# The last 64 tokens of a PEER layer leave the dense down product for gathered value rows

## The chip, the cores and the metric

The kernel runs on one core of a Trainium2 chip, as one launch. The metric is the time of one execution on the device in microseconds (us). The host lays the inputs out by tiles before the launch and is not timed.

## The reference, cut to what matters

Two layers work on 512 tokens of width 1024. Each layer is a convolution and pooling mixer, then a PEER layer: every token picks 8 x 16 = 128 of 16384 one-neuron experts, and its result is the weighted sum of their value rows.

```python
best_v, best_j = lax.top_k(comb, PEER_TOPK)            # 16 per head, 8 heads
idx = (i1 * N_KEYS + i2).astype(jnp.int32)             # expert numbers, 0..16383
gate = jax.nn.softmax(best_v, axis=-1)
...
a = jnp.einsum("tmd,td->tm", u_tab[ib], xb)            # activation of each picked expert
wgt = gb * jax.nn.gelu(a, approximate=False)
return jnp.einsum("tm,tmd->td", wgt, v_tab[ib])        # sum of 128 weighted value rows
```

## The kernel before, in words

The kernel computes the PEER layer densely. The 16384 experts are 128 chunks of 128. In the **up stage** each chunk's tile of `u` (128 x 1024, 512 KB) is multiplied with all 512 tokens; ScalarE applies GELU and stores the result, `[128 experts, 512 tokens]`, in DRAM (`ga_dram`). In the **down stage** each chunk's activations come back, are multiplied with a gate matrix that is zero wherever a token didn't pick the expert, and the product with the chunk's tile of `v` is added up in the eight PSUM banks, one for each 128 of the 1024 output columns.

All of these products are in split precision. A float32 operand is a high half (`_hi`, rounded to fp32r) and a low half (`_lo`, the rest), and a product is three matmuls: high x high, high x low, low x high. So one chunk is 24 matmuls of 128 x 128 weights against 512 tokens: 16 with `w_hi` (L439 in the up stage, L563 in the down stage) and 8 with `w_lo` (L443, L567). The last chunk of a down stage is at L586. ScalarE makes `w_hi` (helper `hi`, L598), GpSimd or VectorE makes `w_lo` (L782 on GpSimd; L1122 and L1149 on VectorE). The tiles of `u` and `v` arrive in a ring of four buffers (`ring`); `w_hi`, `w_lo`, `v_hi`, `v_lo` have two buffers each.

The up stage has four parts. While VectorE finds the best 16 of each head (`top16`, L1059 to L1063, and the gathers at L1093 to L1096), 40 chunks run (`RETRIEVING`). Eight more follow (`EARLY` is 48), beside which TensorE transposes indices and gates (L531) and VectorE copies them out (L1110 to L1115). In the next 64 chunks (`LATE`) the gate matrix is also built: for each of `TOK` = 8 tokens a chunk, VectorE writes one-hot rows (L1129, L1131), TensorE multiplies them (16 small matmuls at L546), ScalarE copies the result (L740) and stores it in blocks of 64 tokens (`g_dram`, `GBLOCKS` = 8). In these 64 chunks VectorE makes `w_lo` (L1122); in the last 16 chunks GpSimd does.

In the down stage SP issues, for each chunk, the activations (L308, 256 KB), the gates (L309, 256 KB, in runs of 64 tokens, which are 256 B) three chunks ahead (`load_back`), and the tile of `v` (`load_tile`, L260). In layer 0 it also issues the next layer's adaLN weights (L332, 512 KB, two in every round of four chunks, over the first 24 rounds), which VectorE reduces with `modulate` (L832). VectorE works in program order (`weights`): the product of activation and gate (L1140), `v_hi` (L1144), `v_lo` (L1146), `w_lo` (L1149). TensorE may start a chunk when `v_lo` of it is there (semaphore `w_ready`). At a stage's end VectorE adds the banks to `x` (L1167).

## Time and profile before

| | |
|---|---|
| median of 3 runs | 3599.91 us (3596.28 to 3601.85) |
| the profiled execution | 3602.71 us, its span 3600.7 us |
| TensorE matmul busy | 3503.5 us, 97% of the span, 16668 instructions |
| VectorE busy | 2422.0 us, 67% |
| ScalarE busy | 1039.3 us, 29% |
| GpSimd busy | 438.8 us, 12% |
| DMA | 633.62 MB, mean 176 GB/s |

The span is the time between the first and the last recorded instruction. A matmul's recorded duration (389 ns for the forms of a chunk) is from its start to the end of its result, and overlaps the next one's; the pace is the distance of starts, or the length of a run of matmuls in the chain of waits divided by their number. The down stage of layer 0 runs from about 1109 to 1813 us of the span, that of layer 1 from about 2884 to 3579 us.

### The profile page before, as it was taken

Reading aid. Unit: us, or ns where it says so; the run is one execution under the profiler, and the core shown is the slowest. Engines: PE = TensorE matmul, PEld = TensorE weight load, DVE = VectorE, ACT = ScalarE, POOL = GpSimd, SP = SyncE. Lnnn points to the kernel's source line nnn. Section 1 sums busy time; section 2 is a strip of 40 time slices with the busy share of each in tenths; the row PEclk is TensorE's granted clock in tenths of the full one; section 3 lists DMA queues with packets and bytes.
Section 4 is the critical chain, followed back from the end, with each engine's and each line's share of the span. In section 5 each row is a group of like instructions: output and inputs, shape, how many; then the busy total and the mean of one; then the engine's idle time right before and its main releaser. Section 6 shows DMA issues by size and latency. Waiting matters only on the chain.

```text
span 3600.7 us, 56122 instructions
## 1 busy us (share of the span) xinstructions
PE 3503.5 (97%) x16668; PEld 2836.9 (79%) x16668; DVE 2422.0 (67%) x6622; ACT 1039.3 (29%) x1382; POOL 438.8 (12%) x186
## 2 busy tenths in 40 slices
PE   5999999999999999999999999999999999999998
PEld 3578888888887888888875788888888888888886
DVE  6973996999924666665577159969999055555555
ACT  3333223444432212121242332234444312121122
POOL 0033443000031000000001334410000400000000
PEclk8999999999999999999999999999999999999999
DMA  6152443555547777786621224435555566666663
GB/s 221 58 215 90 146 143 138 186 199 216 216 181 222 243 235 243 243 244 195 181 93 37 78 97 143 146 132 216 216 181 204 204 204 193 193 192 195 190 196 119
DMA packets 442868, 633.62 MB, mean 176 GB/s; under 512 B 285984, under 2 KB 286368, under 8 KB 440352
## 3 DMA queue, kind: packets, MB, share of 16 engines
q1 hardware_dynamic: 402752, 495.60, 43.5%
q10 hardware_dynamic: 40032, 137.07, 9.7%
q8 instruction: 32, 0.52, 0.1%
q14 instruction: 52, 0.43, 0.0%
HBM read 496.26 MB, written 136.31 MB: 176 GB/s over the span
## 4 chain that ended last, share of the span: by engine, by line
PE 78%; DVE 16%; issue 3%; DMA 1%; ACT 1%; DVEq 0%; SPq 0%; ACTq 0%
PE bank L563 26%; PE bank L439 22%; PE bank L567 13%; PE bank L443 11%; PE bank L546 3%; DVE z_pad L1095 2%; DVE h L1060 2%; DVE h L1063 2%; DVE h L1062 1%; DVE h L1059 1%; DVE scratch L969 1%; DVE z_pad L1093 1%; DVE h L1096 1%; DVE u_pad L1061 1%; PE bank L362 1%
## 5 line engine op out<-in xcount | busy, mean ns | idle before, releaser
L598 ACT ACTIVATE w_hi<-ring 128x1024 fp32r<-128x1024 f32 x584 | 618.9, 1060 | 2243.0 <-PE bank L567 1110.7
L439 PE MATMUL bank<-h_hi,w_hi 128*128 128x512 f32 x2528 | 1000.3, 396 | 5.1 <-ACT scratch L598 2.3
L439 PE MATMUL bank<-h_lo,w_hi 128*128 128x512 f32 x2528 | 985.8, 390 | 0.0
L563 PE MATMUL bank<-v_hi,w_hi 128*128 128x512 f32 x2032 | 792.1, 390 | 5.7 <-DVE v_lo L1146 5.7
L563 PE MATMUL bank<-v_lo,w_hi 128*128 128x512 f32 x2032 | 791.8, 390 | 0.0
L782 POOL TENSOR_TENSOR w_lo<-ring,w_hi 128x1024 fp32r<-128x1024 f32 x172 | 437.1, 2543 | 1717.1 <-ACT w_hi L598 1717.1
L443 PE MATMUL bank<-h_hi,w_lo 128*128 128x512 f32 x2528 | 624.2, 389 | 0.0
L439 PEld LDWEIGHTS bank<-h_hi,w_hi 128*128 128x128 f32 x2528 | 474.8, 188 | 105.1 <-ACT w_hi L598 4.9
L443 PEld LDWEIGHTS bank<-h_hi,w_lo 128*128 128x128 f32 x2528 | 474.5, 188 | 98.5
L439 PEld LDWEIGHTS bank<-h_lo,w_hi 128*128 128x128 f32 x2528 | 474.9, 188 | 97.2 <-issue 1.4
L1131 DVE TENSOR_SCALAR h<-iota_b,keys 128x128 f16<-128x128 f16 x2048 | 543.5, 308 | 0.0
L567 PE MATMUL bank<-v_hi,w_lo 128*128 128x512 f32 x2032 | 501.8, 389 | 0.0
L1144 DVE CAST v_hi<-scratch 128x512 fp32r<-128x512 f32 x256 | 109.2, 427 | 580.7 <-PE bank L567 555.3
L563 PEld LDWEIGHTS bank<-v_hi,w_hi 128*128 128x128 f32 x2032 | 382.5, 188 | 85.8 <-DVE v_lo L1146 6.2
L563 PEld LDWEIGHTS bank<-v_lo,w_hi 128*128 128x128 f32 x2032 | 382.1, 188 | 79.3
L567 PEld LDWEIGHTS bank<-v_hi,w_lo 128*128 128x128 f32 x2032 | 381.4, 188 | 79.2
L1149 DVE TENSOR_TENSOR w_lo<-ring,w_hi 128x1024 fp32r<-128x1024 f32 x256 | 313.7, 1225 | 0.0
L1140 DVE TENSOR_TENSOR scratch<-scratch 128x512 f32<-128x512 f32 x256 | 175.1, 684 | 156.5 <-DMA scratch<-g_scratch 156.5
L1129 DVE TENSOR_SCALAR h<-iota_b,keys 128x128 f16<-128x128 f16 x1024 | 253.4, 247 | 0.0
L1122 DVE TENSOR_TENSOR w_lo<-ring,w_hi 128x1024 fp32r<-128x1024 f32 x128 | 156.7, 1224 | 68.8 <-ACT w_hi L598 68.7
L1146 DVE TENSOR_TENSOR v_lo<-scratch,v_hi 128x512 fp32r<-128x512 f32 x256 | 177.3, 692 | 8.8
L740 ACT ACTIVATE scratch<-bank 128x512 f32<-128x512 f32 x256 | 139.1, 596 | 82.1 <-ACT norm_tmp L710 82.1
(147 smaller groups left out, 1990.9 us busy)
## 6 DMA issues: line engine op xcount, KB each, us to landing
ring<-u_t SPq DMA_DIRECT2D x256, 512.0 KB, 3.3
ring<-v_t SPq DMA_DIRECT2D x256, 512.0 KB, 3.4
ga_scratch<-norm_tmp ACTq DMA_DIRECT2D x256, 256.0 KB, 2.0
g_scratch<-scratch ACTq DMA_DIRECT2D x16, 4096.0 KB, 13.4
scratch<-ga_scratch SPq DMA_DIRECT2D x256, 256.0 KB, 3.8
scratch<-g_scratch SPq DMA_DIRECT2D x256, 256.0 KB, 4.2
scratch<-ada_t SPq DMA_DIRECT2D x76, 512.0 KB, 5.3
ring<-wq_t SPq DMA_DIRECT2D x32, 512.0 KB, 3.4
```

Of the source, the lines that this page charges most:

```text
L439: pe.matmul(to, w_hi[:, b, k * P:(k + 1) * P], part_h[:, k, :], start=(k == 0 and part_h is h_hi), stop=False)
L443: mm = pe.matmul(to, w_lo[:, b, k * P:(k + 1) * P], h_hi[:, k, :], start=False, stop=(k == KC - 1))
L563: pe.matmul(bank[:, k, :], w_hi[:, b, k * P:(k + 1) * P], part_w[:, b, :], start=(first and part_w is v_hi), stop=False)
L567: mm = pe.matmul(bank[:, k, :], w_lo[:, b, k * P:(k + 1) * P], v_hi[:, b, :], start=False, stop=False)
L598: return act.activation(to, of, ACT.Copy)
L782: pool.tensor_tensor(w_lo[:, n % 2, :], ring[:, n % RING, :], w_hi[:, n % 2, :].bitcast(F32), ALU.subtract).then_inc(tile_used[n % RING], 1)
L1122: dve.tensor_tensor(w_lo[:, b, :], ring[:, s, :], w_hi[:, b, :].bitcast(F32), ALU.subtract)\
L1129: dve.tensor_scalar(hot2[:, b, j, :], iota_b[:, :], i2_t[:, col], None, ALU.is_equal)
L1131: ins = dve.tensor_scalar(hot1[:, b, j, q, :], iota_b[:, :], i1_t[:, col], g_part[:, col], ALU.is_equal, ALU.mult)
L1140: dve.tensor_tensor(ga_in[:, s, :], ga_in[:, s, :], g_in[:, s, :], ALU.mult).then_inc(w_step, 1)
L1146: dve.tensor_tensor(v_lo[:, b, :], ga_in[:, s, :], v_hi[:, b, :].bitcast(F32), ALU.subtract)\
L1149: dve.tensor_tensor(w_lo[:, b, :], ring[:, s, :], w_hi[:, b, :].bitcast(F32), ALU.subtract)\
```

## The change

The last 64 tokens (`OWN`) leave the gate matrix and the down product, which keep the other `TD` = 448. They stay in the up stage. Their 64 x 128 picks are laid over 128 partitions and 64 turns (`TURNS`): a turn holds one pick for each of 64 tokens on partitions 0 to 63 and another on 64 to 127. For each turn GpSimd issues two indirect DMAs: `fetch_cells` brings 128 activations of 4 B from `ga_dram`, `fetch_rows` 128 value rows of 4 KB from `v`, into three row buffers that lie in `u_pad` and `z_pad`. VectorE weighs three turns' activations with their gates (`weigh`) and adds row times weight into `own_y` (`add`, one instruction of 128 x 1024 a turn), three turns in a round of four chunks, in rounds 9 to 29 and one more. At the end one matmul for each bank with the constant `fold` adds the two halves of the partitions into the bank's last 64 columns.

With it go these edits: 56 instead of 64 chunks with gates (`LATE`), and seven gate blocks; in the last 24 chunks of the up stage VectorE makes `w_lo` instead of GpSimd; `v_hi` is made by ScalarE (`split_v`); VectorE takes the product of activation and gate one chunk earlier (`step`); the loads of activations run four chunks ahead, and the gates of two chunks come with one DMA, in runs of 512 B; the adaLN loads start in round 1 instead of 0; VectorE computes the rows' and cells' numbers behind the retrieval, and ScalarE lays them out with six small DMAs between the early chunks and those with gates. GpSimd's loop over the layers is written out.

```diff
     RETRIEVING = 10 * N_U // 32
-    EARLY, LATE = RETRIEVING + 2 * RING, N_U // 2
-    TOK = T // LATE
+    OWN = 64
+    TD = T - OWN
+    PICKS = HEADS * TOPK
+    PER_ROW = P // OWN
+    TURNS = PICKS // PER_ROW
+    ROWS = 3
+    TOK = 8
+    EARLY, LATE = RETRIEVING + 2 * RING, TD // TOK
     GTOK = 64
-    GBLOCKS = T // GTOK
+    GBLOCKS = TD // GTOK
+    G_OF = [(GBLOCKS + 1) // 2, GBLOCKS // 2]
+    ADD_FIRST = 9
+    ADD_LAST = ADD_FIRST + TURNS // ROWS
+    assert TURNS % ROWS == 1
+    ADA_AT = 1
...
+        fold = sb("fold", [P, OWN])
+        row_base = sb("row_base", [P, 1])
+        own_token = sb("own_token", [P, 1])
...
-        ga_in = part(0, RING).rearrange("p (s t) -> p s t", t=T)
-        g_in = part(RING, RING).rearrange("p (s t) -> p s t", t=T)
-        i1_t, i2_t, ghi_t, glo_t = (keys[:, n * T:(n + 1) * T] for n in range(4))
+        ga_in = part(0, RING)[:, 0:RING * TD].rearrange("p (s t) -> p s t", t=TD)
+        g_in = part(RING, RING)[:, 0:RING * TD].rearrange("p (s b t) -> p s b t", s=2, b=GBLOCKS)
+        own_y = part(28, 2)
+        v_rows = v_t.rearrange("l e p d -> (l e p) d")
+        ga_cells = ga_dram.rearrange("e p t -> (e p t)").unsqueeze(1)
+        u_flat, z_flat = (t[:, :, :].rearrange("p c t -> p (c t)") for t in (u_pad, z_pad))
+        own_rows = [u_flat[:, 0:D], u_flat[:, D:2 * D], z_flat[:, 0:D]]
+        picked = [z_flat[:, D + n * PICKS:D + (n + 1) * PICKS] for n in range(3)]
+        i1_t, i2_t, ghi_t, glo_t = (keys[:, n * T:n * T + TD] for n in range(4))
+        own_i, own_e, own_g, own_w = (keys[:, n * T + TD:(n + 1) * T] for n in range(4))
...
+                    if n % 2:
+                        pair = n // 2 % 2
+                        sp.dma_start(g_in[:, pair, :, :], g_dram[:, :, bass.ds(RING * first + (n - 1), 2), :]
+                                     .rearrange("b p c t -> p b (c t)")).then_inc(g_landed[pair], 16)
+                    sp.dma_start(ga_in[:, slot, :], ga_dram[c][:, 0:TD]).then_inc(ga_landed[slot], 16)
...
-                for n in range(RING - 1):
+                for n in range(RING):
...
-                            load_back(r, s + RING - 1)
+                            load_back(r, s + RING)
...
-                            pe.matmul(bank[:, k, :], w_hi[:, b, k * P:(k + 1) * P], part_w[:, b, :],
+                            pe.matmul(bank[:, k, 0:TD], w_hi[:, b, k * P:(k + 1) * P], part_w[:, b, 0:TD],
                                       start=(first and part_w is v_hi), stop=False)
                     wait_lo(pe, l, r, stages["v"] + s)
                     for k in range(KC):
-                        mm = pe.matmul(bank[:, k, :], w_lo[:, b, k * P:(k + 1) * P], v_hi[:, b, :],
+                        mm = pe.matmul(bank[:, k, 0:TD], w_lo[:, b, k * P:(k + 1) * P], v_hi[:, b, 0:TD],
                                        start=False, stop=False)
...
+                pe.wait_ge(own_done, l + 1)
                 for k in range(KC):
                     for w_part, v_part in ((w_hi, v_hi), (w_hi, v_lo), (w_lo, v_hi)):
-                        mm = pe.matmul(bank[:, k, :], w_part[:, b, k * P:(k + 1) * P], v_part[:, b, :],
-                                       start=False, stop=(w_part is w_lo))
-                    mm.then_inc(down_done, 1)
+                        pe.matmul(bank[:, k, 0:TD], w_part[:, b, k * P:(k + 1) * P], v_part[:, b, 0:TD],
+                                  start=False, stop=(w_part is w_lo))
+                    pe.matmul(bank[:, k, TD:T], own_y[:, k * P:(k + 1) * P], fold[:, :], start=True, stop=True)\
+                      .then_inc(down_done, 1)
                 pe.nop(nofuse=True).then_inc(chunk_done, 1)
             for k in range(KC):
...
+                act.wait_ge(own_ready, l + 1)
+                for half in range(PER_ROW):
+                    for own, of in zip((own_i, own_e, own_g), picked):
+                        act.dma_start(own[half * OWN:(half + 1) * OWN, :], of[P - OWN:P, half * TURNS:(half + 1) * TURNS])\
+                           .then_inc(own_spread, 16)
...
+                gate_block(GBLOCKS // 2, 0)
...
+                def split_v(r, n):
+                    b = n % 2
+                    act.wait_ge(w_step, N_V * l + RING * r + (n + 1))
+                    wait_product(act, l, r, stages["v"] + n - 2)
+                    copy(v_hi[:, b, 0:TD], ga_in[:, n % RING, :]).then_inc(v_high, 1)
+                split_v(0, 0)
+                split_v(0, 1)
+                def high_rounds(start, end):
+                    with act.Fori(start, end) as r:
+                        for s in range(RING):
+                            split_v(r, s + 2)
+                            hi(r, stages["v"] + s + 2)
...
-                with pool.Fori((stages["u"] + EARLY + LATE) // RING, stages["v"] // RING) as r:
-                    for s in range(RING):
-                        lo(r, s)
+                pool.wait_ge(own_spread, 96 * l + 96)
+                def fetch_rows(n):
+                    pool.wait_ge(rows_used, TURNS * l + n + 1)
+                    pool.indirect_dma_start(own_rows[n % ROWS], None, v_rows,
+                                            bass.IndirectOffsetOnAxis(ap=own_i[:, n:n + 1].bitcast(U32), axis=0))\
+                        .then_inc(rows_landed[n % ROWS], 16)
+                def fetch_cells(n):
+                    pool.wait_ge(w_ready, N_V * l + RING * (ADD_FIRST - 1 + n // ROWS) + (n % ROWS + 2 + RING))
+                    pool.indirect_dma_start(own_w[:, n:n + 1], None, ga_cells,
+                                            bass.IndirectOffsetOnAxis(ap=own_e[:, n:n + 1].bitcast(U32), axis=0))\
+                        .then_inc(cells_landed[n % ROWS], 16)
+                for s in range(RING):
+                    pool.wait_ge(ga_stored[s], 16 * (N_U // RING) * l + 16 * (N_U // RING) + 16)
+                for n in range(TURNS):
+                    fetch_cells(n)
+                    fetch_rows(n)
...
+                row_f, cell_f = rest[:, 512:512 + PICKS], rest[:, 768:768 + PICKS]
+                link(dve.scalar_tensor_tensor(row_f, i1_f[:, TT - 1, :], float(P), i2_f[:, TT - 1, :], ALU.mult, ALU.add))
+                count(dve.tensor_scalar(cell_f, row_f, float(T), own_token[:, 0:1], ALU.mult, ALU.add))
+                link(dve.tensor_scalar(row_f, row_f, row_base[:, 0:1], None, ALU.add))
+                count(dve.tensor_copy(picked[0].bitcast(U32), row_f))
+                count(dve.tensor_copy(picked[1].bitcast(U32), cell_f))
+                count(dve.tensor_scalar(row_base[:, :], row_base[:, :], float(N_U * P), None, ALU.add))
+                dve.wait_ge(gate_ready, l + 1)
+                link(dve.tensor_copy(picked[2], gate[:, TT - 1, :]))
+                dve.nop().then_inc(own_ready, 1)
...
+                def weigh(n, slots):
+                    for s in range(slots):
+                        dve.wait_ge(cells_landed[s], 16 * OF_SLOT[s] * l + 16 * n + 16)
+                    cols = bass.ds(ROWS * n, slots)
+                    dve.tensor_tensor(own_w[:, cols], own_w[:, cols], own_g[:, cols], ALU.mult).then_inc(own_weighed, 1)
+                def add(n, s):
+                    dve.wait_ge(rows_landed[s], 16 * OF_SLOT[s] * l + 16 * n + 16)
+                    dve.wait_ge(own_weighed, WEIGHED * l + n + 2)
+                    dve.wait_ge(rows_used, TURNS * l + ROWS * n + (ROWS + s))
+                    dve.scalar_tensor_tensor(own_y, own_rows[s], own_w[:, bass.ds(ROWS * n + s, 1)], own_y,
+                                             ALU.mult, ALU.add).then_inc(rows_used, 1)
+                with dve.Fori((EARLY + LATE) // RING, N_U // RING) as r:
+                    for s in range(RING):
+                        wait_hi(dve, l, r + stages["u"] // RING, s)
+                        dve.tensor_tensor(w_lo[:, s % 2, :], ring[:, s, :], w_hi[:, s % 2, :].bitcast(F32), ALU.subtract)\
+                           .then_inc(tile_used[s], 1)
+                for b in range(2):
+                    dve.wait_ge(g_stored[b], 16 * G_OF[b] * l + 16 * G_OF[b] + 16)
+                dve.memset(own_y, 0.0).then_inc(own_weighed, 1)
                 def weights(r, s):
+                    dve.wait_ge(ga_landed[s % RING], 16 * (N_V // RING) * l + 16 * r + (16 * (s // RING) + 16))
+                    dve.wait_ge(g_landed[s // 2 % 2], 16 * (N_V // RING) * l + 16 * r + (16 * (s // RING) + 16))
+                    ga = ga_in[:, s % RING, :].rearrange("p (b t) -> p b t", t=GTOK)
+                    dve.tensor_tensor(ga, ga, g_in[:, s // 2 % 2, :, s % 2 * GTOK:(s % 2 + 1) * GTOK], ALU.mult)\
+                       .then_inc(w_step, 1)
+                def low_halves(r, s):
...
+                    dve.wait_ge(v_high, N_V * l + RING * r + (s + 1))
+                    dve.tensor_tensor(v_lo[:, b, 0:TD], ga_in[:, s, :], v_hi[:, b, 0:TD].bitcast(F32), ALU.subtract)\
                        .then_inc(w_ready, 1)
                     wait_hi(dve, l, r + stages["v"] // RING, s)
                     dve.tensor_tensor(w_lo[:, b, :], ring[:, s, :], w_hi[:, b, :].bitcast(F32), ALU.subtract)\
                        .then_inc(tile_used[s], 1)
-                def rounds(start, end, with_ada):
+                def step(r, s, with_ada, own, last=False):
+                    low_halves(r, s)
+                    if not last:
+                        weights(r, s + 1)
+                    if own:
+                        own(r, s)
+                    if with_ada and s < ADA_STEP:
+                        wait_ada(dve, ada_landed, 16, l, s, r - ADA_AT)
+                        modulate(s, ADA_STEP * (r - ADA_AT) + s)
+                def rounds(start, end, with_ada, own):
                     with dve.Fori(start, end) as r:
                         for s in range(RING):
-                            weights(r, s)
-                            if with_ada and s < ADA_STEP:
-                                wait_ada(dve, ada_landed, 16, l, s, r)
-                                modulate(s, ADA_STEP * r + s)
+                            step(r, s, with_ada, own)
...
+                def late_add(r, s):
+                    if s < ROWS:
+                        if s == 0:
+                            weigh(r - ADD_FIRST, ROWS)
+                        add(r - ADD_FIRST, s)
+                def some_rounds(with_ada):
+                    rounds(ADA_AT, ADD_FIRST, with_ada, None)
+                    rounds(ADD_FIRST, ADA_AT + ADA_ROUNDS, with_ada, late_add)
+                weights(0, 0)
+                rounds(0, ADA_AT, False, None)
                 with dve.If(l < LAST):
-                    rounds(0, ADA_ROUNDS, True)
+                    some_rounds(True)
                 with dve.Else():
-                    rounds(0, ADA_ROUNDS, False)
-                rounds(ADA_ROUNDS, N_V // RING, False)
+                    some_rounds(False)
+                rounds(ADA_AT + ADA_ROUNDS, ADD_LAST, False, late_add)
+                weigh(TURNS // ROWS + 0 * l, TURNS % ROWS)
+                add(TURNS // ROWS + 0 * l, 0)
+                dve.wait_ge(rows_used, TURNS * l + TURNS + ROWS)
+                dve.nop().then_inc(own_done, 1)
+                rounds(ADD_LAST, N_V // RING - 1, False, None)
+                for s in range(RING):
+                    step(N_V // RING - 1, s, False, None, s == RING - 1)
```

## Rows read from the trace of the kernel before

**Rows 1.** The page, part 1: busy time of each engine.

```profile
PE 3503.5 (97%) x16668; PEld 2836.9 (79%) x16668; DVE 2422.0 (67%) x6622; ACT 1039.3 (29%) x1382; POOL 438.8 (12%) x186
```

**Rows 2.** The page, part 4: the chain that ended last, by line.

```profile
PE bank L563 26%; PE bank L439 22%; PE bank L567 13%; PE bank L443 11%; PE bank L546 3%; DVE z_pad L1095 2%; DVE h L1060 2%; DVE h L1063 2%; DVE h L1062 1%; DVE h L1059 1%; DVE scratch L969 1%; DVE z_pad L1093 1%; DVE h L1096 1%; DVE u_pad 
```

**Rows 3.** Windows: length, busy PE, PEld, DVE, ACT, POOL; granted clock; DMA share; GB/s.

```profile
620.00:1020.00 400.00, 400.00 (x2483) 327.90 (x2483) 375.17 (x1542) 163.16 (x248) 2.41 (x1) 1.00 0.53 196
1200.00:1300.00 100.00, 100.00 (x443) 82.81 (x442) 65.90 (x95) 19.35 (x19) 0.00 (x0) 1.00 0.79 245
2900.00:3500.00 600.00, 600.00 (x2649) 496.82 (x2648) 318.50 (x443) 117.91 (x111) 0.00 (x0) 1.00 0.66 195
```

**Rows 4.** Chain of waits, one chunk of the down stage: start us, us, what.

```profile
1144.73 3.63 PE bank L563 x16
1148.35 1.81 PE bank L567 x8
```

**Rows 5.** Chain of waits, one chunk with gates of the up stage.

```profile
628.70 3.73 PE bank L439 x16
632.42 1.81 PE bank L443 x8
634.23 0.91 PE bank L546 x16
```

**Rows 6.** Timeline: matmuls of 128 columns, float16 (L546) and float32 (L511).

```profile
614.74 1.07 PE L546 MATMUL bank<-h 128*128 128x128 f16 x16
...
329.56 6.63 PE L511 MATMUL bank<-keys,scratch 128*128 128x128 f32 x57 [1.63 <-ACT scratch L598]
...
329.56 2.53 PEld L511 LDWEIGHTS bank<-keys,scratch 128*128 128x128 f32 x22 [2.05 <-ACT scratch L598]
```

**Rows 7.** VectorE by line, 1128 to 1640 us: busy, mean ns, idle before.

```profile
L1149 DVE TENSOR_TENSOR w_lo<-ring,w_hi 128x1024 fp32r<-128x1024 f32 x94 | 115.2, 1225 | 0.0
...
L1140 DVE TENSOR_TENSOR scratch<-scratch 128x512 f32<-128x512 f32 x94 | 64.4, 685 | 0.0
L832 DVE SCALAR_TENSOR_TENSOR scratch<-scratch,cond 128x1024 f32<-128x1024 f32 x46 | 56.2, 1222 | 18.5 <-DMA scratch<-ada_t 18.5
```

**Rows 8.** DMA issues, 1128 to 1640 us: count, KB, median us to landing.

```profile
scratch<-ada_t SPq DMA_DIRECT2D x46, 512.0 KB, 5.3
```

**Rows 9.** The page, part 5: ScalarE's copies.

```profile
L598 ACT ACTIVATE w_hi<-ring 128x1024 fp32r<-128x1024 f32 x584 | 618.9, 1060 | 2243.0 <-PE bank L567 1110.7
L740 ACT ACTIVATE scratch<-bank 128x512 f32<-128x512 f32 x256 | 139.1, 596 | 82.1 <-ACT norm_tmp L710 82.1
```

**Rows 10.** Timeline of the change from up to down stage, layer 0.

```profile
1109.12 1.06 ACT L598 ACTIVATE w_hi<-ring 128x1024 fp32r<-128x1024 f32 x1 [3.90 <-PE bank L443]
...
1110.09 0.58 ACT L710 ACTIVATE norm_tmp<-bank 128x512 f32<-128x512 f32 x1
...
1110.83 0.34 ACTq L712 DMA_DIRECT2D ga_scratch<-norm_tmp  x1
...
1120.25 0.79 PE L563 MATMUL bank<-v_hi,w_hi 128*128 128x512 f32 x1 [5.74 <-DVE v_lo L1146]
```

**Rows 11.** Chain and timeline: TensorE after an idle time.

```profile
1120.25 6.32 PE bank L563 x16
...
1826.04 2.08 PE L374 MATMUL bank<-norm_tmp,ones 128*128 128x128 f32 x8 [3.46 <-DVE norm_tmp L866]
```

**Rows 12.** Windows at the kernel's start, DMA alone sets the pace; columns as in rows 3.

```profile
14.00:22.00 8.00, 7.87 (x12) 3.37 (x13) 3.50 (x6) 3.71 (x8) 0.00 (x0) 1.00 1.01 397
22.00:30.00 8.00, 1.91 (x5) 0.57 (x3) 6.30 (x11) 0.00 (x0) 0.00 (x0) 0.77 0.95 329
```

**Rows 13.** Timeline of GpSimd, beside a busy VectorE: start us, us.

```profile
548.03 2.40 POOL L782 TENSOR_TENSOR w_lo<-ring,w_hi 128x1024 fp32r<-128x1024 f32 x1 [3.04 <-ACT w_hi L598]
553.48 4.13 POOL L782 TENSOR_TENSOR w_lo<-ring,w_hi 128x1024 fp32r<-128x1024 f32 x1 [3.04 <-ACT w_hi L598]
```

**Rows 14.** Waits: us in total, times, longest.

```profile
DVE keys L1110 <- PE bank L531: 27.2, 2, 13.6
```

More of the change, by code:

```diff
@@ L767, in _ @@
             pool.tensor_copy(iota_b[:, :], iota_i).then_inc(consts_made, 1)
-            with pool.Fori(0, DEPTH) as l:
+            pool.memset(row_base[:, :], 0.0).then_inc(consts_made, 1)
+            pool.wait_ge(consts_made, 3)
+            pool.iota(iota_i[:, 0:1], [[1, 1]], base=T - P, channel_multiplier=1).then_inc(pool_step, 1)
+            pool.wait_ge(pool_step, 3)
+            pool.tensor_copy(own_token[:, :], iota_i[:, 0:1]).then_inc(consts_made, 1)
+            for l in range(DEPTH):
                 pool.wait_ge(x_new, 2 * KC * l + KC)
-                settle(pool)
                 pool.memset(u_pad[:, :, 0:UPAD], 0.0)
@@ L809, in _ @@
             dve.wait_ge(dve_step, 2)
+            dve.wait_ge(const_landed, 32)
+            dve.tensor_tensor(fold[:, :], ident[:, 0:OWN], ident[:, OWN:P], ALU.add).then_inc(dve_step, 1)
+            dve.wait_ge(dve_step, 3)
             dve.wait_ge(x_landed, 16)
             dve.nop().then_inc(x_new, KC)
-            FIRST = 2
+            FIRST = 3
             for s in range(RING):
@@ L1133, in _ @@
                         ins.then_inc(hot_ready, 1)
[L1136 to L1146 removed]
+                WEIGHED = 1 + (TURNS + ROWS - 1) // ROWS
@@ new lines, in _ @@
+                OF_SLOT = [TURNS // ROWS + (s < TURNS % ROWS) for s in range(ROWS)]
+                def weigh(n, slots):
[9 more added lines that the diff above has]
+                                             ALU.mult, ALU.add).then_inc(rows_used, 1)
```

89 lines of the change are left out of this document (43 added, 46 removed).

## The prediction

> **What bounds the kernel now.** I read the page's totals first: TensorE is busy 97% of the span, VectorE 67% [rows 1]. Then the chain of waits by line: 39% lies on the down stage's matmuls (L563, L567) and 33% on the up stage's [rows 2], so the columns that leave are on the path. Then the windows: in three stretches that cover both stages TensorE never stops and its clock is 1.00; VectorE is at 66% and 53% in the down stages, at 94% in the chunks with gates; the DMA share is 0.79 beside the adaLN loads and 0.66 without [rows 3]. Last the chain inside a chunk: 3.63 + 1.81 = 5.44 us for 24 matmuls, 226.7 ns each [rows 4]; a chunk with gates takes 3.73 + 1.81 + 0.91 = 6.45 us, 1.01 us more [rows 5]. TensorE is the bound in both stages, so the question is what a matmul of 448 columns costs, and which engine or queue catches up.
>
> **Term 1, 64 columns less.** Two layers x 128 chunks x 24 = 6144 matmuls. At the granted clock of 1.00 (2.4 GHz) one column a cycle is 213.3 ns for 512; the row shows 226.7, 13.3 more. If the 13.3 are fixed, 448 columns take 200.0 ns, a chunk 4.80 us, and the saving is 6144 x 26.7 ns = 163.8 us. If the pace follows the line through the 128-column form (0.91 us for 16, 56.9 ns) [rows 5], a column is (226.7 - 56.9)/384 = 0.442 ns, the saving 28.3 ns each, 174 us. Against it stands the weight load: a load is recorded with 187 ns (82.81 us for 442 [rows 3]), just what 448 columns stream in (187). But the float32 form of 128 columns runs at 6.63/57 = 116 ns, its loads at 2.53/22 = 115 [rows 6], so a load of this size can be hidden in 115 ns and isn't the limit at 200. I take **-163.8**, ends 0 (pace stays) and -174.
>
> **Term 2, gates.** 64 - 56 = 8 chunks a layer lose their gate work: 16 x 1.01 = **-16.1 us**. VectorE keeps its load a chunk (94% busy, 6.0 of 6.45 us) [rows 3], so TensorE stays ahead there and nothing more comes of it. In the 24 last chunks VectorE's `w_lo` costs 1.22 us [rows 7] in 5.44, hidden.
>
> **Term 3, from up to down.** Before, chunk 0 starts at once and chunk 1 waits 5.74 us, behind `modulate` of layer 0's first adaLN tile, and then runs its 16 matmuls in 6.32 instead of 3.63 us, at half clock [rows 10, 11]: 8.4 us, which go, since adaLN begins a round later. What is late next: `v_hi` of chunk 0 now stands on ScalarE behind the last GELU. From the row at 1109.12, when TensorE has just run out: `w_hi` and GELU end at 1110.67, the store is issued by 1111.17 [rows 10], the copy takes 0.53 (596 ns for 512 [rows 9]), `v_lo` 0.62: TensorE starts about 1112.4, idle 3.3 us. After an idle time of 3.46 us the clock was low (8 small matmuls in 2.08 us) [rows 11], so I add 2.5 us; ends 0 and 2.7. In layer 0 5.8 - 8.4, in layer 1 +5.8: **+3.2 us**, between -1.8 and +3.6.
>
> **Term 4, fold.** 8 matmuls of 64 float32 columns a layer, each between half and all of the 116 ns form [rows 6]: 16 x 0.06 to 0.12, **+1.2 us**, on the path.
>
> **What is meant to be hidden.** A round of four chunks is 19.2 us.
> VectorE: at 1.055 ns a column ((1225 - 685)/512) a two-input form of 448 columns takes 618 ns. Four times 618 + 618 + 1225 is 9.8 us, three adds of the L832 form 3.7, `weigh` 0.1, two `modulate` 2.5: 16.1 us, 84% [rows 7]. Following one round in order, VectorE is at most 1 us behind its nominal place, and `v_lo` may be 3.7 us late before TensorE waits. Cost 0; without that cover, each us a round more than 19.2 costs 16 us.
> ScalarE: 1.06 + 0.53 us of 4.80 [rows 9]. Its six small DMAs are 6 x 0.34 = 2.0 us [rows 10] once a layer, in a chunk of 5.44 us with 1.6 us of copies. Cost 0.
> VectorE's seven instructions behind the retrieval have at most 128 columns, each under the 0.69 us of a 512-column form [rows 7]: under 5 us in the 13.6 in which it waits for the transposes [rows 14]. Cost 0.
> SP issues less: two gate loads a round instead of four. The activations' loads get a chunk more of lead.
>
> **Term 5, DMA.** Engine time a chunk before: 0.66 x 5.44 = 3.59 us in layer 1, 0.79 x 5.44 = 4.30 in layer 0 [rows 3]. The difference, 0.71, is adaLN's 256 KB a chunk; so 512 KB take 1.42, a chunk's activations 0.71, and its gates, 1024 pieces of 256 B, the remaining 1.46. After: tile 1.42, activations 0.62, gates (448 pieces of 512 B) between 0.64 at the same time a piece and 1.28 at the same time a byte, rows 3/4 x 1.42 = 1.06, cells 96 pieces 0.14: 3.88 to 4.52 us, under 4.80. In layer 0's rounds 9 to 24 adaLN's 0.71 comes on top: 4.59 to 5.23. That is 64 chunks x 0 to 0.43 = 0 to 27 us. The same by bytes: 1.64 MB a chunk at 397 or 329 GB/s, which the kernel's start reached [rows 12], is 4.1 or 5.0 us, 0 to 12. I take **+5**.
> *DMA: Bandwidth & Descriptors* in the Trainium skill, section on where 436 GB/s comes from, says that loads from HBM are bound near 358 GB/s for each core. By that figure the crowded chunk takes 4.6 us and Term 5 is 0; the trace went past it (397 GB/s), so the rule isn't the limit here.
>
> **Unknown: GpSimd's indirect DMAs.** No row shows one. Per turn there are two calls, three turns a round, so a call may take 19.2/6 = 3.2 us before it sets the pace. Nearest rows: an issue on another queue 0.34 us [rows 10], GpSimd's own big subtraction 2.40, and 4.13 when VectorE is busy beside it [rows 13]. I take about 1.3, nearer to the issue, since a call handles 128 indices and not 128 x 1024 elements: hidden, 0 us; the ends are 0.34 (0 us) and 4.13 (+238, below). Landing: the last cells of a round are asked for at `v_lo` of its chunk 3. `weigh` comes a chunk later (4.8 us) and behind the wait for `w_hi`, `w_lo` and a product (2.4 us), and may slip another 2.9 before TensorE starves: 10 us from asking. In the crowded part of layer 0 a load of 512 KB lands in 5.3 us [rows 8]. Cost 0.
>
> **Sum.** -163.8 - 16.1 + 3.2 + 1.2 + 5 = -170.5. The profiled execution, 3602.7 us, becomes 3432.2; it lies 2.8 above the runs' median, so 3429.
>
> **Rivals.**
> *GpSimd sets the pace (this one ends slower).* If a call takes p > 3.2 us, VectorE waits in its program order for rows, TensorE behind it, and each layer grows by 64 x (2p - 6.4) us. At p = 4.13 that is 2 x 119 = 238 us: 3667. The gain is eaten at p = 3.9. For: the 4.13 us row, and VectorE 84% busy, mostly with two-input instructions. Against: 2.40 when it is let through.
> *SBUF — State Buffer* in the Trainium skill, section "Who interferes with whom", says that a VectorE instruction with two inputs in SBUF blocks a GpSimd instruction that reads SBUF until it is done. By that rule each call's index read may wait for up to one instruction; the trace agrees (2.40 against 4.13). One wait of 1.22 us on top of 1.3 stays under 3.2.
> *Weight loads hold the pace.* The matmuls stay at 226.7 ns because a load of fp32r weights, not the columns, sets it. For: a recorded load is as long as 448 columns. Against: rows 6. Then only terms 2 to 4 count, and DMA is slack: 3599.9 - 11.7 = 3588.
> *DMA saturates in layer 0.* The upper end of Term 5: 3451.
> *Cells come late.* Each us beyond 10 us from issue to landing costs 22 rounds x 2 = 44 us; at 12 us 3517. For: they queue behind 512 KB rows in a full layer-0 DMA. Against: the 5.3 us of a load of 512 KB [rows 8].
>
> **How the numbers follow.** Forecast with up to 10 us of Term 5: 0.70. DMA saturated 0.12. GpSimd's pace 0.09 (0.06 of it slower, 0.03 a lesser gain). Weight loads 0.06, mostly a partial hold between. Cells late 0.03. Less than 0.2% (7 us) can't be told from no change here. Faster 0.93, within 0.01, slower 0.06. The range starts at Term 1's other end with nothing for Term 3 and 5 (3411) and goes a little below for the hand-over; upward it takes in saturated DMA and some of a waiting VectorE: 3406 to 3478.
>
> **What would show it.** In the chain, L563 x16 at 3.20 us and L567 x8 at 1.60 (3.63 would be the weight loads). L546 count 1792. TensorE idle before L563 of about 3.3 us once a layer. GpSimd's calls in pairs every 6.4 us or less; idle VectorE before the adds released by a DMA would be the GpSimd or the cell rival. DMA share 0.95 or more in rounds 9 to 24 of layer 0, 0.8 to 0.95 in layer 1. The prediction is wrong if a chunk of layer 1's rounds 9 to 29 takes over 4.9 us.

## The result, and the profile after

| | before | after |
|---|---|---|
| median of the runs | 3598.99 us (3596.28 to 3601.85) | 3479.56 us (3476.11 to 3486.53) |
| ratio | | 0.9671, interval 0.9656 to 0.9686 |
| the profiled execution | 3602.71 us, span 3600.7 | 3476.11 us, span 3473.6 |
| down stage, layer 0 | 1108.92 to 1815.45: 706.5 us | 1101.6 to 1765.4: 663.8 us |
| down stage, layer 1 | 2883.89 to 3580.38: 696.5 us | 2822.1 to 3453.2: 631.1 us |

The change saves 119 us of the 171 forecast. L563 is now L593, L567 is L597 and L546 is L576. The page of the kernel after, busy time and the chain by line, against [rows 1, 2]:

```profile
PE 3354.8 (97%) x16444; PEld 2831.6 (82%) x16444; DVE 2422.4 (70%) x6203; ACT 1141.7 (33%) x1606; POOL 688.3 (20%) x413
...
PE bank L469 23%; PE bank L593 19%; PE bank L473 11%; PE bank L597 9%; DMA scratch<-ada_t 4%; PE bank L576 3%; DVE z_pad L1180 2%; DVE h L1145 2%; DVE h L1148 2%; DVE h L1147 1%; DVE h L1144 1%; DVE w_lo L1274 1%; DVE scratch L1054 1%; DVE 
```

The down stage's matmuls fell from 39% of the chain to 28%. New in the chain is `DMA scratch<-ada_t` with 4%: a transfer that the forecast took as hidden. The windows (start and end, length, busy PE, PEld, DVE, ACT, POOL with the number of instructions, granted clock, DMA share, GB/s) say where: layer 0's rounds with adaLN and adds, its last rounds, and layer 1:

```profile
1295.00:1640.00 345.00, 326.32 (x1559) 296.38 (x1558) 244.72 (x319) 98.96 (x130) 140.75 (x98) 0.98 0.87 305
1640.00:1757.00 117.00, 117.00 (x568) 106.28 (x567) 72.53 (x89) 35.46 (x47) 22.98 (x20) 1.00 0.70 236
...
3000.00:3300.00 300.00, 300.00 (x1482) 278.00 (x1481) 206.17 (x249) 93.84 (x123) 106.81 (x92) 1.00 0.84 282
```

In layer 1 TensorE never stops: 300/1482 = 202.4 ns a matmul, a chunk of 4.86 us. In layer 0 it stands still for 18.7 of 345 us, and the DMA engines aren't full there (0.87). The waits of the kernel after (us in total, times, longest) name the chain behind it:

```profile
DVE scratch L917 <- DMA scratch<-ada_t: 53.9, 33, 4.1
DVE keys L1240 <- DMA keys<-ga_scratch,keys: 36.0, 16, 3.5
PE bank L593 <- DVE v_lo L1271: 26.0, 13, 3.7
```

And one round of it, in the timeline of SP, VectorE and ScalarE (start, us, line, [idle before, released by]):

```profile
1405.57 1.09 SPq L361 DMA_DIRECT2D scratch<-ada_t  x2
...
1411.51 0.17 DVE L1240 TENSOR_TENSOR keys<-keys  x1 [3.17 <-DMA keys<-ga_scratch,keys]
...
1415.18 1.23 DVE L917 SCALAR_TENSOR_TENSOR scratch<-scratch,cond 128x1024 f32<-128x1024 f32 x1 [2.08 <-DMA scratch<-ada_t]
...
1418.75 0.58 ACT L630 ACTIVATE v_hi<-scratch 128x448 fp32r<-128x448 f32 x1 [7.34 <-DVE scratch L1264]
```

SP asks for the round's two adaLN tiles at 1405.57. VectorE first waits 3.17 us for gathered cells, then another 2.08 for the first of the tiles, which it can use 9.6 us after it was asked for. The product of the next chunk (L1264) stands behind both in VectorE's order, `v_hi` (idle 7.34 us) behind the product, `v_lo` behind `v_hi`, TensorE behind `v_lo`. The DMA issues of 1300 to 1600 us (count, KB, median us to landing) show that everything lands late, where [rows 8] had 5.3 (and the kernel after itself 5.7 from 1100 to 1280 us, where it hardly gathers yet):

```profile
ring<-v_t SPq DMA_DIRECT2D x56, 512.0 KB, 8.7
scratch<-ada_t SPq DMA_DIRECT2D x28, 512.0 KB, 9.1
...
keys<-ga_scratch,keys POOLq DMA_INDIRECT x42, 7.2
```

### The profile page after: what moved, and what is told of

The parts are those of the page before. It is cut to its first block, busy times and chain, and to the rows that moved or that the text cites. A ratio compares the mean times of both kernels' runs of the same rounds, so it can differ in the third digit from the quotient of the medians.

```text
span 3473.6 us, 55467 instructions
## 1 busy us (share of the span) xinstructions
PE 3354.8 (97%) x16444; PEld 2831.6 (82%) x16444; DVE 2422.4 (70%) x6203; ACT 1141.7 (33%) x1606; POOL 688.3 (20%) x413
## 4 chain that ended last, share of the span: by engine, by line
PE 69%; DVE 19%; DMA 5%; issue 5%; ACT 1%; SPq 1%; DVEq 0%; ACTq 0%
PE bank L469 23%; PE bank L593 19%; PE bank L473 11%; PE bank L597 9%; DMA scratch<-ada_t 4%; PE bank L576 3%; DVE z_pad L1180 2%; DVE h L1145 2%; DVE h L1148 2%; DVE h L1147 1%; DVE h L1144 1%; DVE w_lo L1274 1%; DVE scratch L1054 1%; DVE z_pad L1178 1%; DVE h L1181 1%
## 5 line engine op out<-in xcount | busy, mean ns | idle before, releaser
L593 PE MATMUL bank<-v_hi,w_hi 128*128 128x448 f32 x2032 | 751.6, 370 | 26.1 <-DVE v_lo L1271 26.0
L593 PE MATMUL bank<-v_lo,w_hi 128*128 128x448 f32 x2032 | 749.5, 369 | 0.0
L473 PE MATMUL bank<-h_hi,w_lo 128*128 128x512 f32 x2528 | 624.3, 389 | 0.0
L473 PEld LDWEIGHTS bank<-h_hi,w_lo 128*128 128x128 f32 x2528 | 474.5, 188 | 98.6
L469 PEld LDWEIGHTS bank<-h_lo,w_hi 128*128 128x128 f32 x2528 | 474.9, 188 | 97.4 <-issue 1.4
L845 POOL TENSOR_TENSOR w_lo<-ring,w_hi 128x1024 fp32r<-128x1024 f32 x140 | 360.1, 2574 | 789.6 <-ACT w_hi L630 789.6
L866 POOL DMA_INDIRECT keys<-ga_scratch,keys x128 | 155.4, 1214 | 1812.8 <-DVE v_lo L1271 1807.9
L1227 DVE TENSOR_SCALAR h<-iota_b,keys 128x128 f16<-128x128 f16 x1792 | 482.9, 316 | 0.0
L597 PE MATMUL bank<-v_hi,w_lo 128*128 128x448 f32 x2032 | 454.2, 366 | 0.0
L630 ACT ACTIVATE v_hi<-scratch 128x448 fp32r<-128x448 f32 x256 | 148.2, 579 | 883.2 <-PE bank L597 749.8
L593 PEld LDWEIGHTS bank<-v_hi,w_hi 128*128 128x128 f32 x2032 | 386.2, 190 | 64.0 <-DVE v_lo L1271 32.2
L593 PEld LDWEIGHTS bank<-v_lo,w_hi 128*128 128x128 f32 x2032 | 386.4, 190 | 32.0
L597 PEld LDWEIGHTS bank<-v_hi,w_lo 128*128 128x128 f32 x2032 | 381.8, 188 | 31.4
L1271 DVE TENSOR_TENSOR v_lo<-scratch,v_hi 128x448 fp32r<-128x448 f32 x256 | 159.9, 625 | 321.7 <-ACT v_hi L630 321.5
L1274 DVE TENSOR_TENSOR w_lo<-ring,w_hi 128x1024 fp32r<-128x1024 f32 x256 | 313.6, 1225 | 64.7 <-ACT w_hi L630 64.4
L1225 DVE TENSOR_SCALAR h<-iota_b,keys 128x128 f16<-128x128 f16 x896 | 228.3, 255 | 0.0
L1253 DVE TENSOR_TENSOR w_lo<-ring,w_hi 128x1024 fp32r<-128x1024 f32 x48 | 58.8, 1226 | 198.6 <-ACT w_hi L630 198.6
L1218 DVE TENSOR_TENSOR w_lo<-ring,w_hi 128x1024 fp32r<-128x1024 f32 x112 | 137.4, 1227 | 63.0 <-ACT w_hi L630 62.9
```

The source lines that it names most:

```text
L469: pe.matmul(to, w_hi[:, b, k * P:(k + 1) * P], part_h[:, k, :], start=(k == 0 and part_h is h_hi), stop=False)
L473: mm = pe.matmul(to, w_lo[:, b, k * P:(k + 1) * P], h_hi[:, k, :], start=False, stop=(k == KC - 1))
L593: pe.matmul(bank[:, k, 0:TD], w_hi[:, b, k * P:(k + 1) * P], part_w[:, b, 0:TD], start=(first and part_w is v_hi), stop=False)
L597: mm = pe.matmul(bank[:, k, 0:TD], w_lo[:, b, k * P:(k + 1) * P], v_hi[:, b, 0:TD], start=False, stop=False)
L630: return act.activation(to, of, ACT.Copy)
L845: pool.tensor_tensor(w_lo[:, n % 2, :], ring[:, n % RING, :], w_hi[:, n % 2, :].bitcast(F32), ALU.subtract).then_inc(tile_used[n % RING], 1)
```

## The experiments

Each median stands against runs of the kernel before on the same chip (3600.3, 3601.6 and 3600.7 us in the three groups of runs). Three groups of questions: what layer 0 loses, what the hand-over costs, what a column is worth.

**Layer 0: bytes or lead.** `e1_modulate_later` is the kernel after with the two `modulate` of a round behind chunks 2 and 3 instead of 0 and 1.

```diff
-                    if with_ada and s < ADA_STEP:
-                        wait_ada(dve, ada_landed, 16, l, s, r - ADA_AT)
-                        modulate(s, ADA_STEP * (r - ADA_AT) + s)
+                    if with_ada and s >= RING - ADA_STEP:
+                        m = s - (RING - ADA_STEP)
+                        wait_ada(dve, ada_landed, 16, l, m, r - ADA_AT)
+                        modulate(m, ADA_STEP * (r - ADA_AT) + m)
```

> The changed kernel with one edit: the two modulate steps of a round stand behind chunks 2 and 3 instead of 0 and 1. The bytes, the order in which SP issues the loads and VectorE's work a round stay the same. Of the changed kernel's profile: in layer 0's rounds 9 to 24 a round takes about 21.6 us instead of 19.4, 32 us in all, and the chain runs through the adaLN load (8 to 10 us to landing). Theory A (no lead: SP issues this load only behind the last tile of the round before, and VectorE wants it about 5 us later, so 9 us of landing stop it in program order): the load gets some 10 us more, the rounds go back to 19.4 to 19.8 us, about 3450 us. Theory B (the DMA engines are full in these rounds, share 0.87): the same bytes take the same time, the wait moves to another tile, 3475 to 3485 us.

Measured 3455.11 us (3447.26 to 3471.73), ratio 0.9605 (0.9582 to 0.9627). Its windows:

```profile
1295.00:1640.00 345.00, 345.00 (x1704) 319.77 (x1704) 270.08 (x345) 108.51 (x142) 131.91 (x106) 1.00 0.95 329
...
3000.00:3300.00 300.00, 300.00 (x1454) 272.44 (x1453) 201.65 (x243) 91.70 (x121) 106.25 (x92) 1.00 0.84 278
```

The same bytes pass through the same engines, in layer 0 at 329 GB/s instead of 305 and share 0.95 instead of 0.87, and TensorE doesn't stop: 1704 matmuls instead of 1559, 202.5 ns each. Only the lead of the load, the time from its issue to its use, grew by two chunks: the pair issued at 1391.94 us is used from 1406.67 on, 14.7 us later, where the kernel after wanted it after 7.5 (1405.57 to 1413.10). Its waits in the kernel as a whole, against the three above:

```profile
DVE scratch L917 <- DMA scratch<-ada_t: 10.7, 10, 4.2
PE bank L593 <- DVE v_lo L1271: 7.4, 2, 3.7
DVE keys L1240 <- DMA keys<-ga_scratch,keys: 6.8, 5, 1.8
```

The wait for cells went too, though nothing of it was touched; the two waits of TensorE that are left are the hand-overs. Layer 1 ran slower here, 206.3 ns a matmul instead of 202.4; more on that below.

`e8_load_ahead` gives the lead from the other side: VectorE's order stays, SP issues the adaLN loads of a round within the round before, behind chunks 1 and 2.

```diff
+                def load_ada(q, s):
+                    wait_ada(sp, ada_used, 1, l, s, q)
+                    sp.dma_start(ada[:, s, :], ada_t[(l + 1) % DEPTH, ADA_STEP * q + s]).then_inc(ada_landed[s], 16)
...
-                        for s in range(ADA_STEP if with_ada else 0):
-                            wait_ada(sp, ada_used, 1, l, s, r - ADA_AT)
-                            sp.dma_start(ada[:, s, :], ada_t[(l + 1) % DEPTH, ADA_STEP * (r - ADA_AT) + s])\
-                              .then_inc(ada_landed[s], 16)
                         for s in range(RING):
                             load_back(r, s + RING)
                             load_tile(l, v_t, RING * r + (RING + s), r, stages["v"] + RING + s)
+                            if with_ada and 1 <= s <= ADA_STEP:
+                                load_ada(r - ADA_AT + 1, s - 1)
...
+                    for s in range(ADA_STEP):
+                        load_ada(0, s)
...
```

> The changed kernel with the adaLN loads issued inside the round before, behind chunks 1 and 2, instead of at the start of the round; VectorE's order is the changed kernel's. It gives the load the lead from the other side. Theory A (no lead): as e1, 3450 to 3460 us. If e1's gain came from the better spread of VectorE's work (modulate away from the chunks with adds) and not from the lead, this one stays at 3475 to 3485 us.

Measured 3454.55 us (3443.45 to 3468.05), ratio 0.9598 (0.9575 to 0.962). Its window of layer 0:

```profile
1295.00:1640.00 345.00, 345.00 (x1671) 313.32 (x1670) 262.23 (x340) 105.77 (x139) 134.68 (x104) 1.00 0.90 323
```

No stop either (345/1671 = 206.5 ns, layer 0 at the slower pace). The load issued at 1386.88 us is used at 1402.73, 15.9 us later. Two edits that share nothing but the lead give the same, so the short lead is the cause. The landing itself is faster here, 6.3 us in the median of 1300 to 1600 us instead of 9.1, though more bytes pass (323 GB/s); why it is so long in the kernel after stays open. It isn't the stops alone: the pair issued at 1297.63 us, ahead of the first long stop, landed 8.3 us later.

`e3_no_adaln_fetch` leaves out the adaLN loads of the down stage, `e2_no_row_fetch` the gathered value rows:

```diff
-                            sp.dma_start(ada[:, s, :], ada_t[(l + 1) % DEPTH, ADA_STEP * (r - ADA_AT) + s])\
-                              .then_inc(ada_landed[s], 16)
+                            sp.nop().then_inc(ada_landed[s], 16)
```
```diff
-                    pool.indirect_dma_start(own_rows[n % ROWS], None, v_rows,
-                                            bass.IndirectOffsetOnAxis(ap=own_i[:, n:n + 1].bitcast(U32), axis=0))\
-                        .then_inc(rows_landed[n % ROWS], 16)
+                    pool.nop().then_inc(rows_landed[n % ROWS], 16)
```

> The changed kernel without the adaLN loads of the down stage: SP signals at once, modulate runs on old tiles. Left out: 48 loads of 512 KB in layer 0. VectorE's work is the same. Both DMA theories: rounds 9 to 24 of layer 0 at 19.4 to 19.6 us, about 3447 us. If VectorE's work alone (16.1 us a round) held TensorE up, the time would stay above 3470.

> The changed kernel without its value-row DMAs: GpSimd signals at once, the adds run on what lies in the row buffers. Left out: fetch_rows, 512 KB a turn (64 MB over both layers). The cells are still fetched, VectorE's work is the same. Both theories expect layer 0's 32 us back, since the traffic that fills the engines is gone: about 3447 us. Layer 1 is at 4.86 us a chunk with the rows and should stay there. If the loss stays (3475 or more), neither DMA theory holds and VectorE's added work in its program order is the cause.

Measured 3455.45 us (3453.42 to 3456.23), ratio 0.9599 (0.9586 to 0.9612), without the adaLN loads, and 3444.61 us (3441.81 to 3466.62), 0.9595 (0.9568 to 0.9621), without the rows. Taking out the bytes of adaLN brings what e1 brings by moving the instruction that uses them, so the bytes themselves cost nothing once the lead is there. Without the rows the short lead is enough: the adaLN load lands in 5.5 us (median of 1300 to 1600 us) instead of 9.1. The rows make the landing late, and the lead decides whether that costs anything. Their windows of layer 0, without adaLN and without rows:

```profile
1295.00:1640.00 345.00, 345.00 (x1704) 319.78 (x1703) 268.33 (x345) 108.19 (x143) 139.07 (x106) 1.00 0.84 283
```
```profile
1295.00:1640.00 345.00, 345.00 (x1704) 319.68 (x1703) 267.63 (x345) 108.54 (x142) 70.37 (x53) 1.00 0.74 249
```

`e4_cells_first` tried the rival of late cells: the three cell fetches of a turn of rows go behind chunk 1's `v_lo`, ahead of the row fetches.

```diff
-                    pool.wait_ge(w_ready, N_V * l + RING * (ADD_FIRST - 1 + n // ROWS) + (n % ROWS + 2 + RING))
+                    pool.wait_ge(w_ready, N_V * l + RING * (ADD_FIRST - 1 + n // ROWS) + (2 + RING))
...
-                for n in range(TURNS):
-                    fetch_cells(n)
-                    fetch_rows(n)
+                for first in range(0, TURNS, ROWS):
+                    turns = range(first, min(first + ROWS, TURNS))
+                    for n in turns:
+                        fetch_cells(n)
+                    for n in turns:
+                        fetch_rows(n)
```

> The changed kernel with GpSimd's order changed: in each round the three cell fetches are issued first, all behind chunk 1's v_lo, then the three row fetches. The bytes stay. Theory A in its narrow form (the adaLN load alone): weigh's wait for cells (36 us in all) goes, but the adaLN wait behind it grows by as much, 3470 to 3480 us. Theory C (the cells' landing is what costs, since the last cells of a round are asked for only a chunk and a half ahead): 3450 to 3460 us.

Measured 3485.12 us (3483.3 to 3492.19), ratio 0.9683 (0.9669 to 0.9696): no gain over the kernel after, whose ratio has an interval that overlaps this one. Its waits (of its slowest run, 3492.19 us, which is the one profiled):

```profile
DVE scratch L920 <- DMA scratch<-ada_t: 97.4, 32, 6.5
PE bank L593 <- DVE v_lo L1274: 31.0, 17, 3.7
```

The wait for cells is no longer in the list, and the wait for adaLN took its place (97.4 us instead of 53.9). The cells were in front of the same late load; they weren't the limit.

**The hand-over.** `e7_handover` is e1 with `v_hi` of chunk 0 ahead of the last GELU and its store on ScalarE; for that the last round of the up stage leaves the loop.

```diff
-                with act.Fori((EARLY + LATE) // RING, N_U // RING) as r:
+                with act.Fori((EARLY + LATE) // RING, N_U // RING - 1) as r:
...
-                split_v(0, 0)
+                for s in range(RING):
+                    if s == RING - 1:
+                        split_v(0, 0)
+                    hi(N_U // RING - 1, stages["u"] + s + 2)
+                    gelu(N_U // RING - 1, s)
```

> The kernel with modulate two chunks later (e1_modulate_later) and one more edit: ScalarE makes v_hi of the down stage's chunk 0 before the last GELU of the up stage instead of behind it. In the changed kernel TensorE is idle 3.7 us there and then runs its first 16 matmuls in 6.1 to 6.2 us instead of 3.24, in each layer. If v_hi's place is the cause, both go: 2 x (3.7 + 1.7 to 2.9) = 11 to 13 us less than e1's 3455, about 3443 us. If v_lo of chunk 1 is then late as well, half of it.

Measured 3433.12 us (3431.59 to 3434.13), ratio 0.9536 (0.9523 to 0.9549), the fastest full version here. The chain of waits at layer 0's hand-over, first of the kernel after, then of e7:

```profile
1104.16 0.58 ACT v_hi L630
1104.75 0.02 issue
1104.77 0.64 DVE v_lo L1271
1105.41 0.04 issue
1105.45 6.18 PE bank L593 x16
1111.63 1.62 PE bank L597 x8
1113.25 3.24 PE bank L593 x16
1116.49 1.62 PE bank L597 x8
```
```profile
1097.18 1.81 PE bank L473 x8
1099.00 3.24 PE bank L593 x16
1102.24 1.62 PE bank L597 x8
```

In the kernel after, TensorE ran out at 1101.77 (the last row of `L473` starts at 1099.94 and takes 1.83), stood 3.7 us, and then did 16 matmuls in 6.18 us instead of 3.24. Both are gone in e7: 2 x (3.7 + 2.9) = 13.2 us against the kernel after. From e1's median it is 22.0 us. In e1's own trace the 16 matmuls took 5.06 us in layer 0 and 4.93 in layer 1 (3.24 and 3.31 in the chunks behind), so its hand-overs cost 2 x 3.7 + 3.4 = 10.8 us, and 11 are left.

The rest is a pace that e1 had and e7 hadn't (206.3 against 202.4 ns in layer 1: 3072 x 3.9 = 12 us). `e9_short_stall` is e7 with a stop of TensorE at the start of round 1:

```diff
+                pe.wait_ge(w_ready, N_V * l + RING + 2 + RING)
+                settle(pe)
```

> The kernel e7_handover with one wait more: at the start of round 1 of each down stage TensorE waits until v_lo of chunk 5 is there instead of chunk 4, some 1.3 us. e7's five runs lay within 3 us (3431.6 to 3434.1), while the kernels in which TensorE stops at the hand-over spread over some 25 us in steps of about 12.5 (e8: 3443.5, 3454.6, 3455.6, 3468.1), and their stages show either 202 or 206.3 ns a matmul. Theory P (the 448-column form has two paces, and which one a stage gets is drawn when TensorE starts again after a stop): the runs spread again, in steps of 13 us, from 3436 up to 3462. If the stop has nothing to do with it, all runs lie within 3 to 4 us of 3436.

Measured 3433.3, 3439.28, 3447.83, 3448.14 and 3449.3 us, where e7's five runs lie within 2.5; ratio 0.9559 (0.9541 to 0.9577). The run profiled is one of the slower (3447.83 us); its chain in layer 1, before the added stop, behind it and late in the stage, and then layer 0 right behind its stop:

```profile
2801.37 3.24 PE bank L593 x16
2804.61 1.63 PE bank L597 x8
...
2808.01 3.57 PE bank L593 x16
2811.57 1.65 PE bank L597 x8
2813.22 3.31 PE bank L593 x16
...
3001.70 3.31 PE bank L593 x16
3005.01 1.65 PE bank L597 x8
```
```profile
1121.54 3.50 PE bank L593 x16
1125.04 1.62 PE bank L597 x8
1126.66 3.25 PE bank L593 x16
```

Layer 1 runs at 202.9 ns a matmul up to the added stop and at 206.7 behind it, to the end of the stage; layer 0 stays at 202.9. So the stop is where the pace changed. Other traces agree. In layer 0 of the kernel after, a chunk takes 4.86 us up to the crowded rounds and between most stops in them, but 4.96 from the stop at 1607 us on, to the end. In e4's layer 0 it changes from one to the other eight times between 1307 and 1593 us, each time behind a stop. Many stops leave it as it was. The stop itself costs little (1.8 us each), and the time moved by up to 16 us.

**What a column is worth.** The kernel before, with nothing changed but the columns of the down stage's matmuls: 480, 448, 416 and 384.

```diff
-                            pe.matmul(bank[:, k, :], w_hi[:, b, k * P:(k + 1) * P], part_w[:, b, :],
+                            pe.matmul(bank[:, k, 0:448], w_hi[:, b, k * P:(k + 1) * P], part_w[:, b, 0:448],
```

> The kernel before with one edit: the down product's 24 matmuls a chunk run over 448 columns. Left out: the last 64 tokens' retrieval in both layers, with nothing in its place. It measures the columns alone. The changed kernel's chain has 3.24 us for 16 matmuls, 202.5 ns each, in layer 1, and two of the first experiments had 206.3 ns there throughout. If the pace belongs to the form, this kernel runs at 202.5 or 206.3 ns and ends at 3600.3 - 6144 x (226.7 - 202.5 to 206.3) = 3452 to 3475 us. If the added loads, GpSimd and ScalarE's v_hi slowed TensorE, it runs at the forecast's 200.0 ns, 3436 us.

> The same with 384 columns (left out: the last 128 tokens' retrieval). Three laws of the pace: one column a cycle and a fixed 13.3 ns gives 173.3 ns, 3272 us; the step seen from 512 to 448 (24.2 ns less) again gives 178.3 ns, 3303 us; weight loads that bind give 188 ns or more, 3362 us and up. DMA needs about 4.3 of 4.2 to 4.3 us a chunk in layer 0, so the pace is read from layer 1.

> The kernel before with the down product's matmuls at 480 columns (left out: the last 32 tokens' retrieval). 512 columns run at 226.7 ns and 384 at 173.2 to 173.3 (columns at 2.4 GHz and 13.3 ns); 448 run at 202.0 or 206.3, not at the 200.0 of that law. If 448 is an exception, 480 columns run at 213.3 ns and the time is 3519 us; if the law bends over the whole range, at 215 to 217 ns, 3530 to 3540 us.

> The same with 416 columns (left out: the last 96 tokens' retrieval). By the law with 13.3 ns on top 186.7 ns, 3355 us and some us of DMA waits in layer 0; if the columns between 384 and 512 carry more, as 448 do, 189 to 193 ns, 3370 to 3395 us.

Chain of waits in layer 1, of 480, 448, 416 and 384 columns, one chunk each:

```profile
3001.65 3.47 PE bank L563 x16
3005.12 1.73 PE bank L567 x8
```
```profile
3003.59 3.25 PE bank L563 x16
3006.84 1.62 PE bank L567 x8
```
```profile
3001.12 2.99 PE bank L563 x16
3004.11 1.49 PE bank L567 x8
```
```profile
3000.14 2.77 PE bank L563 x16
3002.91 1.39 PE bank L567 x8
```

| columns | median, us (range) | ratio (interval) | ns a matmul | over columns/2.4 |
|---|---|---|---|---|
| 512 | 3600.73 | | 226.7 | 13.3 |
| 480 | 3538.91 (3537.46 to 3539.29) | 0.9826 (0.9811 to 0.9841) | 216.7 | 16.7 |
| 448 | 3456.29 (3455.07 to 3458.75) | 0.9599 (0.9585 to 0.9614) | 202.9 or 206.7 | 16.2 or 20.0 |
| 416 | 3365.26 (3363.77 to 3369.73) | 0.9349 (0.9335 to 0.9363) | 186.7 | 13.3 |
| 384 | 3312.87 (3308.55 to 3314.28) | 0.9203 (0.9189 to 0.9217) | 173.3 | 13.3 |

The pace is (first + second row)/24, whose rounding is 0.4 ns; counts in windows give 202.0 to 202.5 for 448. (The second value of 448 is from e9's rows above.) The medians of 416 and 384 lie 10 and 41 us above the times expected from these paces (3355 and 3272 us): there TensorE also waits for `v_lo`, 7.8 and 30.8 us in all. The paces are read from stretches without such a wait. The weight loads hold no floor up here: 384 columns run at 173.3 ns, below the 188 that a load is recorded with in that same stretch. The 13.3 ns over the columns are the same at 512, 416 and 384, and more at 480 and 448.

## Why the prediction missed

The median of 3479.56 us lies above the forecast of 3429, and 1.6 above the end of the range. The direction, the bound (TensorE) and the mechanism of terms 1 to 3 were right. By its own terms, in the profiled executions (-126.6 us):

| term | forecast | measured | from |
|---|---|---|---|
| 1, columns | -163.8 | -149.3 | 6144 x (226.7 - 202.4) |
| 2, gates | -16.1 | -16.1 | L576, 1792 instead of 2048 |
| 3, hand-over | +3.2 | +4.8 | 2 x (3.7 + 2.9) - 8.4 |
| 4, fold | +1.2 | +3.4 | 16 x 0.21 |
| 5, DMA in layer 0 | +5 | +31.5 | layer 0's matmuls less layer 1's |
| sum | -170.5 | -125.7 | -126.6 in the trace |

**Term 5 is the step that failed**, by 26 of the 44 us. It priced the crowded rounds as engine time ("4.59 to 5.23" us a chunk, at most 27 us in all) and so by throughput. Throughput wasn't short: e1 put the same bytes through at 329 GB/s with no stop. What the profile showed, and the working didn't use, is in [rows 7]: the row of L832 has 18.5 us of idle time before it, released by the adaLN DMA. SP issues the round's two tiles only when the last tile of the round before is dealt with, and VectorE wants the first some 5 to 8 us later (5.4 for the pair of 1278.10 us, 7.5 for that of 1405.57). With a landing of 5.3 us that would do or nearly do; at 9.1 it doesn't. The forecast weighed the landing time for the cells (10 us of slack) and not for the one load with no lead. The 31.5 us in parts: 18.7 of standstill in the window; 10.6 because its matmuls took 326.32/1559 = 209.3 ns instead of 202.5 (the granted clock is 0.98 there; behind the stop of 2.3 us that ends at 1373.67 it was 0.54 from 1374 to 1376, and 16 matmuls took 5.1 us instead of 3.24); 2 at the 206.0 ns of the last rounds. A round took 21.46 us instead of 19.4.

**Term 1's mechanism was right, its size off by 15 us.** Time goes with the columns, not with the weight loads; e6 and e11 rule the weight-load rival out. But "If the 13.3 are fixed" doesn't hold at 448 columns: it holds at 416 and 384. The other end of the term (-174) was further off still: the line through the float16 form doesn't describe this one.

**Terms 2 and 3 held.** [Rows 5] gave the gates exactly. The idle time at the hand-over is 3.7 us where 3.3 was worked out, the slow clock behind it 2.9 where 2.5 was. ScalarE's six small DMAs took 4.08 us (at 612.17) where 2.0 were worked out, and stayed hidden.

**Term 4 counted half of its work.** It is on the path, as forecast. In the chunk with the fold one 128-row block of outputs takes 0.82 us in layer 0 and 0.84 in layer 1, instead of 0.62 and 0.61, so 0.20 to 0.23 us for a float32 matmul of 64 columns, above the upper bound of 0.12. The trace has two records for each such matmul:

```profile
1758.28 0.33 PE L619 MATMUL bank<-fold,scratch 128*128 128x64 f32 x2
```

The 116 ns of [rows 6] are the pace of records of the same kind: the program has 128 matmuls at L511, the trace of the kernel before 256 records. With two records a matmul the term's own 0.06 to 0.12 us give 1.9 to 3.8 us, and the 3.4 lie inside.

**The rivals.** GpSimd's calls never set the pace. Its rows of 1300 to 1600 us (count | busy, mean ns | idle before, released by) show it waiting for VectorE, not the other way round:

```profile
L866 POOL DMA_INDIRECT keys<-ga_scratch,keys x42 | 68.5, 1631 | 166.7 <-DVE v_lo L1271 162.4 <-issue 4.3
L859 POOL DMA_INDIRECT u_pad<-v_t,keys x28 | 39.9, 1425 | 8.5 <-issue 8.5
L859 POOL DMA_INDIRECT z_pad<-v_t,keys x14 | 13.2, 946 | 4.3 <-issue 4.3
```

A call takes 0.95 to 1.63 us in the mean, against 1.3 taken and 3.2 allowed. By the rule of *SBUF — State Buffer*, "Who interferes with whom", in the Trainium skill, a call that reads its indices from SBUF could be held up by one VectorE instruction with two inputs in SBUF; the spread of these means, 0.68 us, leaves room for it and doesn't show it. "Cells come late" was half seen: they landed in 7.2 us and VectorE did wait for them, 36.0 us, but only together with the adaLN tile (e1: 6.8 us, e4: none and no gain). "DMA saturates" had the right place and the wrong mechanism, and its 27 us would have been short by 4.5.

**What the change costs apart from its gain.** Dense 448 columns alone run at 3456.3 us. Less the 16.1 of the gates and of the 8.5 that layer 0's chunk 1 loses in it (6.4 of waiting, then 16 matmuls in 5.34 us instead of 3.24; before: [rows 10, 11]), plus the 3.4 of the fold, that is some 3435; e7, which gathers and adds all the rows, runs at 3433.1. With the lead in place, the path through indexed DMA and VectorE is hidden.

## What to carry to other kernels

Price a DMA that becomes crowded twice: by throughput, and by the landing time of the one load that is used soonest after its issue. Landing times can rise well before the engines are full (5.3 to 9.1 us at a share of 0.87), and the share alone doesn't tell them (e8: 6.3 us at 0.90). A small idle time with a DMA as releaser in the trace of before marked the load that broke here. Then move the use later or the issue earlier, before taking bytes away; and when a stage of an engine that works in program order ends with stores, put the next stage's first operand ahead of them.
